# The first pair of column blocks as four plain products of halves

## The reference

```python
def short_conv_mixer(h, w_in, conv_w, w_out):
    b_gate, c_gate, v = jnp.split(h @ w_in, 3, axis=-1)
    u = c_gate * v
    y = lax.conv_general_dilated(u, conv_w[:, None, :], ...)   # width 3, causal, per channel
    return (b_gate * y) @ w_out

h = rmsnorm(x, mix_norm)
x = x + short_conv_mixer(h, conv_w_in, conv_w, conv_w_out)
a = jax.nn.relu(rmsnorm(x, mlp_norm) @ mlp_w1)
x = x + (a * a) @ mlp_w2
```

## Time and profile before

| what | value |
|---|---|
| three timed runs | 1918.24, 1918.30, 1918.65 us, median 1918.3 us |
| the profiled execution: span from the first instruction to the last | 1916.3 us |
| its own time beside the span | not listed apart; the median of the runs is 2.0 us above the span |
| TensorE busy | 1887.0 us (98%) |
| VectorE, ScalarE busy | 1715.8 us (90%), 1022.4 us (53%) |
| granted TensorE clock, mean | 0.998 |

### The profile page before, as it was taken

One profiled execution on the slowest core, in us unless ns is written; L12 is line 12 of the kernel. 1 busy time (PEld: TensorE's weight loads), 2 busy tenths in 40 slices (PEclk: granted clock), 3 DMA queues, 4 the chain that ended last, 5 costly groups with the idle time before them and its releaser, 6 DMA issues.

```text
span 1916.3 us, 22288 instructions
## 1 busy us (share of the span) xinstructions
PE 1887.0 (98%) x8512; PEld 1560.8 (81%) x8512; DVE 1715.8 (90%) x1518; ACT 1022.4 (53%) x1095; POOL 152.9 (8%) x244
## 2 busy tenths in 40 slices
PE   7899999999999999999999999999999999999999
PEld 5678888888888888888888888888888888888887
DVE  7999899898999989989899898998998889888878
ACT  6653655535557476565665756655444333333332
POOL 1100011000011111111111111110000000000000
PEclk9999999999999999999999999999999999999999
DMA  9865659657776975877858678599988878887782
GB/s 357 313 219 164 219 188 363 218 153 270 250 201 245 370 222 182 332 247 227 328 184 332 247 226 328 184 399 399 357 315 348 350 281 312 351 317 278 294 330 115
DMA packets 120698, 527.90 MB, mean 275 GB/s; under 512 B 13072, under 2 KB 17168, under 8 KB 95504
## 3 DMA queue, kind: packets, MB, share of 16 engines
q1 hardware_dynamic: 86176, 401.64, 54.3%
q0 software_dynamic: 34272, 124.80, 21.4%
q10 hardware_dynamic: 144, 0.04, 0.0%
HBM read 433.10 MB, written 93.32 MB: 275 GB/s over the span
## 4 chain that ended last, share of the span: by engine, by line
PE 94%; DMA 2%; DVE 2%; ACT 1%; issue 1%; POOL 0%; SPq 0%; ACTq 0%; DVEq 0%
PE pair L1097 91%; PE pair L1117 2%; DMA act_kept<-act 1%; DMA raw<-in_turns 1%; DVE ring L839 1%; ACT ring L564 0%; DVE raw L833 0%; DVE sum L870 0%; DVE act L796 0%; ACT quads L513 0%; ACT act L549 0%; DVE quads L898 0%; DVE sum_l_mix L870 0%; ACT later L520 0%; ACT x_tok L524 0%
## 5 line engine op out<-in xcount | busy, mean ns | idle before, releaser
L1097 PE MATMUL pair<-ring,act 128*128 128x512 f32 x8064 | 1851.2, 390 | 23.5 <-DVE ring L839 19.1
L1097 PEld LDWEIGHTS pair<-ring,act 128*128 128x128 f32 x8064 | 1510.5, 188 | 341.3 <-issue 25.8
L564 ACT ACTIVATE ring<-raw 128x1024 fp32r<-128x1024 f32 x672 | 712.1, 1061 | 827.6 <-PE pair L1097 561.8
L839 DVE TENSOR_TENSOR ring<-raw,ring 128x1024 fp32r<-128x1024 f32 x672 | 809.9, 1222 | 149.1 <-ACT ring L564 146.3
L833 DVE TENSOR_TENSOR raw<-raw 128x1024 f32<-128x1024 f32 x324 | 382.0, 1221 | 8.0
L448 POOL DMA_DIRECT2D spill<-stage x136 | 78.4, 611 | 474.9 <-ACT stage L668 371.7
L461 POOL DMA_DIRECT2D raw<-in_turns x60 | 53.6, 1047 | 746.6 <-DVE raw L833 746.6
L820 DVE TENSOR_TENSOR stage<-quads,stage 128x1024 fp32r<-128x1024 f32 x68 | 83.1, 1222 | 25.5 <-ACT stage L668 25.0
L870 DVE TENSOR_TENSOR sum<-pair,sum 128x1024 f32<-128x1024 f32 x64 | 78.0, 1219 | 0.0
L668 ACT ACTIVATE stage<-quads 128x1024 fp32r<-128x1024 f32 x68 | 71.5, 1052 | 11.8 <-DVE quads L756 10.2
L590 ACT ACTIVATE sum<-pair 128x1024 f32<-128x1024 f32 x64 | 64.9, 1013 | 0.2 <-PE pair L1097 0.2
(11 more groups left out here) (93 smaller groups left out, 435.4 us busy)
## 6 DMA issues: line engine op xcount, KB each, us to landing
raw<-in_turns SPq DMA_DIRECT2D x192, 1024.0 KB, 7.1
act<-spill SPq DMA_DIRECT2D x282, 512.0 KB, 6.7
spill<-stage POOLq DMA_DIRECT2D x136, 512.0 KB, 9.2
act<-act_kept SPq DMA_DIRECT2D x68, 512.0 KB, 6.7
raw<-in_turns POOLq DMA_DIRECT2D x60, 512.0 KB, 8.4
act_kept<-act POOLq DMA_DIRECT2D x26, 512.0 KB, 9.0
x_tok<-in_x SPq DMA_DIRECT2D x4, 1024.0 KB, 14.5
x<-mixed SPq DMA_DIRECT2D x8, 512.0 KB, 16.1
```

What stands on the lines that cost most here:

```text
L564: nc.scalar.activation(ring[g % RING][:, 0], raw[:, RAW_OF[j], 2 * (s % 2):2 * (s % 2) + 2, :], ACT.Copy).then_inc(hi_ready, 1)
L839: nc.vector.tensor_tensor(ring[g % RING][:, 1], raw[:, RAW_OF[order(v)[s // 2]], 2 * (s % 2):2 * (s % 2) + 2, :], ring[g % RING][:, 0].bit ...
L1097: mm = nc.tensor.matmul(bank, stationary, moving, start=(opens and k == 0 and n == 0), stop=(closes and k == NT - 1 and n == 2))
```

## The change

Turns 0 and 1 (pair 0) become plain: eight products of quadrants each instead of seven, with no sums on either side. A turn then has 8 slots, one for each half of a weight quadrant in the order R11, R12, R21, R22, and every slot serves two left quadrants: 24 matmuls a slot, 192 a turn. The four results stay in the four PSUM pairs over both turns, and ScalarE copies them out (`copy_plain`) during turn 2. The sums of weights, the T3 transfers, the twelve adds and the five copies of pair 0 go away for turns 0 and 1. The summed left factors are still made, since turns 2 and 3 use them, but later in the order. The first slot is made in pieces: x11 and R11 are loaded in two halves each, and ScalarE and VectorE scale and split them by pieces of one k (`split_lead_hi`, `split_lead_lo`, `split_first_hi`, `split_first_lo`). TensorE runs nine matmuls on a tile of ones before its first product.

```diff
+WARM = 9
+PLAIN_TURNS, PLAIN_SLOTS = 2, 8
+L21 = 7
+PLAIN_RAWS = (R11, R12, R21, R22)
+PLAIN_LEFTS = {R11: (L11, L21), R12: (L11, L21), R21: (L12, L22), R22: (L12, L22)}
+PLAIN_BANK = {(0, 0): 0, (1, 0): 2, (0, 1): 3, (1, 1): 1}
 def t3_by_transfer(v):
-    return v < V_OUT + 2 or V_UP <= v < V_DOWN
+    return PLAIN_TURNS <= v < V_OUT + 2 or V_UP <= v < V_DOWN
...
 # SyncE
-            load_x(quad["L11"], 0, 0, x_in["L11"])
-            load_raw(0, R11)
+            for h in range(2):
+                k = slice(2 * h, 2 * h + 2)
+                sp.dma_start(quad["L11"][:, k], xt_v[:, k, 0:HALF]).then_inc((first_x_in, x_in["L11"])[h], 16)
+                sp.dma_start(raw[:, R11, k, :], turns[R11, :, k]).then_inc((first_raw_in, raw_turn_in[R11])[h], 16)
+                if h == 0:
+                    load_x(quad["L21"], 0, 1, x_in["L21"])
+            load_raw(0, R12)
             load_x(quad["L12"], DT // 2, 0, x_in["L12"])
+            load_x(quad["L22"], DT // 2, 1, x_in["L22"])
             load_raw(0, R21)
-            load_x(quad["L21"], 0, 1, x_in["L21"])
-            load_x(quad["L22"], DT // 2, 1, x_in["L22"])
-            load_raw(0, R12)
             load_raw(0, R22)
...
+            for v in range(PLAIN_TURNS):
+                for n, r in enumerate(PLAIN_RAWS):
+                    sp.wait_ge(lo_ready, first_slot(v) + 2 * n + 2)
+                    load_raw(v + 1, r)
+                    if v == 1 and r == R11:
+                        sp.wait_ge(act_lo_ready, direct_done(0, S4))
+                        for t in (0, 1):
+                            load_tokens(t)
...
 # ScalarE
+            def split_lead_hi(name, k):
+                act.wait_ge(first_x_in if name == "L11" and k < 2 else x_in[name], 16)
+                place = act_place(0, {"L11": L11, "L21": L21}[name])
+                nc.scalar.activation(place[:, 0, k, :], quad[name][:, k, :], ACT.Copy,
+                                     scale=cols[:, MIX + k:MIX + k + 1]).then_inc(lead_hi[name], 1)
+            def split_first_hi(k):
+                act.wait_ge(first_raw_in, 16)
+                nc.scalar.activation(ring[0][:, 0, k, :], raw[:, R11, k, :], ACT.Copy).then_inc((first_hi, hi_ready)[k], 1)
+            def copy_plain(n):
+                act.wait_ge(used, 2 * PLAIN_SLOTS - (2 if n < 2 else 0))
+                if n < 2:
+                    act.wait_ge(squared, 1)
+                o = sums_of(0)[(0, 5, 4, 1)[n]]
+                nc.scalar.activation(o[:], pairs[(0, 2, 3, 1)[n]][:], ACT.Copy).then_inc(plain_copied, 1)
...
+            split_lead_hi("L11", 0)
+            split_first_hi(0)
+            split_lead_hi("L11", 1)
+            split_first_hi(1)
+            split_lead_hi("L21", 0)
+            split_lead_hi("L21", 1)
             split_turn_hi(0, 1)
+            for k in (2, 3):
+                split_lead_hi("L11", k)
+            for k in (2, 3):
+                split_lead_hi("L21", k)
+            split_turn_hi(0, 2)
+            split_turn_hi(0, 3)
             direct_hi(0, L12)
+            direct_hi(0, L22)
+            split_turn_hi(0, 4)
+            direct_hi(0, S3)
+            scale_later(0)
+            split_turn_hi(0, 5)
+            scale_later(1)
+            direct_hi(1, L11)
+            split_turn_hi(0, 6)
+            direct_hi(1, L21)
+            square_tokens(2)
+            split_turn_hi(0, 7)
...
+                    if v == PLAIN_TURNS:
+                        if s == 0:
+                            direct_hi(1, S2)
+                            root_of(1)
+                        if s == 1:
+                            copy_plain(0)
+                            copy_plain(1)
+                        if s == 2:
+                            direct_hi(1, S4)
+                        if s == 3:
+                            copy_plain(2)
+                            copy_plain(3)
...
 # VectorE
+            def split_lead_lo(name, k):
+                dve.wait_ge(lead_hi[name], k + 1)
+                place = act_place(0, {"L11": L11, "L21": L21}[name])
+                nc.vector.scalar_tensor_tensor(out=place[:, 1, k, :], in0=quad[name][:, k, :],
+                                               scalar=cols[:, MIX + k:MIX + k + 1], in1=place[:, 0, k, :].bitcast(F32),
+                                               op0=ALU.mult, op1=ALU.subtract).then_inc(lead_lo[name], 1)
...
+            split_lead_lo("L11", 0)
+            split_first_lo(0)
+            split_lead_lo("L11", 1)
+            split_first_lo(1)
+            split_lead_lo("L21", 0)
+            split_lead_lo("L21", 1)
             split_turn_lo(0, 1)
+            for k in (2, 3):
+                split_lead_lo("L11", k)
+            for k in (2, 3):
+                split_lead_lo("L21", k)
+            split_turn_lo(0, 2)
+            scale_x("L12")
+            split_turn_lo(0, 3)
+            scale_x("L22")
             direct_lo(0, L12)
+            direct_lo(0, L22)
+            scale_x("L11")
+            scale_x("L21")
             direct_form(0, 0)
+            split_turn_lo(0, 4)
+            direct_form(0, 2)
+            direct_lo(0, S3)
+            split_turn_lo(0, 5)
...
+                    if v == PLAIN_TURNS and s == 3:
+                        form_weights(v, T2)
+                        form_u(0, 0)
+                        form_u(0, 1)
...
 # TensorE
+            pe.wait_ge(ones_ready, 1)
+            for _ in range(WARM):
+                nc.tensor.matmul(pairs[3][:, 0, 0:P], ones[:], ones[:], start=True, stop=True)
             pe.wait_ge(ones_ready, 2)
+            for v in range(PLAIN_TURNS):
+                for s in range(PLAIN_SLOTS):
+                    r = PLAIN_RAWS[s // 2]
+                    if v > 0 or s > 0:
+                        pe.wait_ge(lo_ready, PLAIN_SLOTS * v + s + 1)
+                    for left in PLAIN_LEFTS[r]:
+                        if v > 0 or left in (L12, L22):
+                            pe.wait_ge(act_lo_ready, direct_done(v, left))
+                        for k in (2 * (s % 2), 2 * (s % 2) + 1):
+                            if v == 0 and s < 2:
+                                pe.wait_ge(lead_lo[{L11: "L11", L21: "L21"}[left]], k + 1)
+                            if v == 0 and s == 0 and left == L11:
+                                pe.wait_ge((first_lo, lo_ready)[k], 1)
+                            for t in range(2):
+                                mm = plain_tile(v, r, left, k, t)
+                    mm.then_inc(used, 1)
```

More of the change, by code:

```diff
@@ L218, in conv_mlp_layer @@
         ones_ready = sem("ones_ready")
-        x_scaled = sem("x_scaled")
-        x_diagonal_scaled = {n: sem(f"x_diagonal_scaled_{n}") for n in ("L11", "L22")}
+        x_scaled = {n: sem(f"x_scaled_{n}") for n in ("L11", "L21", "L12", "L22")}
+        later_scaled = sem("later_scaled")
+        lead_hi = {n: sem(f"lead_hi_{n}") for n in ("L11", "L21")}
+        lead_lo = {n: sem(f"lead_lo_{n}") for n in ("L11", "L21")}
+        first_x_in = sem("first_x_in")
+        first_raw_in = sem("first_raw_in")
+        first_hi = sem("first_hi")
+        first_lo = sem("first_lo")
+        plain_copied = sem("plain_copied")
         squared = sem("squared")
@@ L261, in formed @@
         def formed(v, t):
-            before = sum(3 if t3_by_transfer(w) else 4 for w in range(v))
+            before = sum(3 if t3_by_transfer(w) else 4 for w in range(PLAIN_TURNS, v))
             return 2 * (before + ({T1: 1, T2: 2, T4: 3}[t] if t3_by_transfer(v) else t))
@@ L394, in _ @@
                 load_tokens(t)
-            for v in range(NV - 1):
+            for v in range(PLAIN_TURNS):
[6 more added lines that the diff above has]
+                            load_tokens(t)
+            for v in range(PLAIN_TURNS, NV - 1):
                 after = v + 1
@@ L413, in _ @@
                     elif r is not None:
-                        sp.wait_ge(lo_ready, SLOTS * v + {R12: 10, R22: 12, R21: 14}[r])
+                        sp.wait_ge(lo_ready, first_slot(v) + {R12: 10, R22: 12, R21: 14}[r])
                         load_raw(after, r)
[L416 to L419, removed]
                     if after == V_DOWN and j in (L11, S1, L12, S3):
@@ L875, in form_u @@
                 o, other = ((first, s4), (l22, s1))[half]
-                dve.wait_ge(added, 12 * q + (11, 12)[half])
+                if q == 0:
+                    dve.wait_ge(plain_copied, (3, 4)[half])
+                else:
+                    dve.wait_ge(added, pair_added(q) + (11, 12)[half])
                 dve.wait_ge(norm_step, NORM_X)
@@ new lines, in _ @@
+            direct_form(1, 2)
+            split_turn_lo(1, 2)
+            split_turn_lo(1, 3)
+            split_turn_lo(1, 4)
+            direct_lo(1, L12)
+            direct_lo(1, L22)
+            split_turn_lo(1, 5)
+            direct_lo(1, S3)
+            split_turn_lo(1, 6)
+            split_turn_lo(1, 7)
+            direct_lo(1, S1)
+            direct_form(1, 1)
+            dve.wait_ge(squared, NT)
```

(17 more changed lines are left out.)

263 lines of the change are left out of this document (131 added, 132 removed).

## The result

The changed kernel takes 1909.02 us (four runs, 1908.8 to 1909.13), the one before 1918.47 on the same chip: 9.45 us less. The measured ratio is 0.9947, 95% interval 0.9934 to 0.9959 (the two medians alone give 0.9951): a small gain, clear of the noise. Forecast were 10.4 us less, 1907.9.

What follows compares the result with a forecast made beforehand. The start was taken as bound by the chain weights, sum, high part, low part, the rest by TensorE's matmul count. Turn 2 starting 10.1 us earlier and 0.3 within it made -10.4: 1918.3 became 1907.9, range 1906 to 1913.5.

Steps and rivals of the forecast that it cites:

- TensorE's count: Turns 0 and 1: 384 matmuls at 0.2267 us take 87.04 us if nothing waits; 48 added matmuls cost 10.9 us.
- The first product: Kernel start: with x11 and R11 in halves, the first product begins at 6.9 us, 2.8 earlier.
- The lower end of the range: First product no earlier than 6.2 us, as a small load takes 3.3 us to land; total 1906.4 with no cold matmul.
- The clock: Start of turn 0: half-clock matmuls cost 0 if the nine on ones serve, 1.4 us if they fail; 0.7 taken.
- rival D: Cold start: slow clock costs 2.7 us in place of 0.7, giving 1909.9 us; chance 0.12.
- my bounds: Before the first product: each matmul on ones takes 0.26 to 0.42 us, nine ending at 3.4 to 4.8.
- The slots behind: Ring slots after the first: tightest is slot 5, ready at 32.7 against 34.1 needed, cover 1.4 us.
- Rival A: Turn 0: the feed is late, one wait at each of slots 4 to 7, +4.2 us, 1912.1; chance 0.15.
- The handover: Turn 2, slot 3: `turn_quad` needs `form_u` 6.3 us after the plain turns end, cover 1.9; turn 2 takes 39.89.
- Rivals B and C: Turns 0 and 1: B, half the waits stay, 1915.9 us, chance 0.08; C, weights' transfers set the waits, 1923.9, 0.07.
- The 18.84 us: Time lost in turns 0 and 1 of the kernel before: some 2.8 us clock, 16 waits.

Runs made afterwards that it cites:

- the first kernel with other first loads: Changed kernel with R11's first two k each alone and first on SyncE's queue, x11's half on ScalarE's, eleven matmuls on ones: 1910.49 us.
- whole first loads: Changed kernel with x11 and R11 each loaded whole in one transfer, splitting by pieces kept: 1910.98 us.
- the kernel with 64 matmuls fewer: Changed kernel with one of three matmuls of each product left out in turn 1 (low left part by high weights): 1899.7 us.
- fourteen: Changed kernel with fourteen matmuls on ones in place of nine before the first product: 1907.61 us.
- The kernel with eight sums: Changed kernel with the first sum of left factors done eight times instead of once on VectorE, before slot 4 of turn 0: 1913.63 us.
- the seven products without sums: Kernel before, seven products, with sums of weights and their T3 transfers left out in turns 0 and 1: 1908.61 us, ratio 0.9944.
- on the seven products: Kernel before with x11 and R11 in halves, first slot split by k, x11's scaling moved behind slot 2: 1920.66 us, ratio 1.0011.

## Why the prediction was right

The mechanism held at each step but for two sizes; both erred to the same side, so no large errors cancel in the total.

- *TensorE's count.* 384 matmuls at 0.2267 with no wait behind the first: right, 43.52 in turn 1.
- *The first product*, forecast at 6.9, came at 7.46. The mis-sized term is the transfer of R11's half, 1.2 us behind x11's half; it measured 2.0 (x11's half came 0.15 earlier and the work 0.1 shorter than said). I had halved the time of a whole transfer; in the same stretch the halves moved at 250 GB/s, the whole transfers at 452, on engines nearly as busy. Smaller packets and x21's share of the stretch both fit; they were not separated. +0.56. The lower end of the range took 3.3 us for a small load "whatever its size"; that is not borne out, the 40 KB of column scales took 3.3, 2.9 and, in the first kernel with other first loads, 4.6.
- *The clock*, taken as 0.7, half of 1.4: it cost 1.43, the upper case named there (rival D's mechanism, though not its 2.7). Half of two cases is no mechanism, and the case that came is the one where the nine fail. The question put as open, whether the idle time behind the matmuls on ones undoes them, has the answer that it can: with 2.2 to 3.5 us idle, seven to eleven matmuls ran at half clock in the two traces of the changed kernel and with whole first loads, none in the kernel with 64 matmuls fewer; fourteen, with 0.23 us idle, cost 0.12. +0.73. The price of the matmuls themselves: nine took 4.21 us and fourteen 6.34, so 0.426 for each of the five more, the upper of my bounds. The Trainium skill ("FP8 and Floating Point Precision", TensorE Precision Notes) says that a true 32-bit product takes four passes; the estimate made from it, 0.42, agrees with this trace, which shows the time and not the passes.
- *The slots behind.* Forecast cover at slot 5 was 1.4 us; the trace has slot 5 ready at 31.6 and TensorE there at 36.1, 4.5 us. TensorE came 2.0 later than said, by the first product (0.56) and the clock (1.43); the lists ran 1.1 shorter, as instructions that take 1.22 follow each other at 1.14 when nothing is waited for. Rival A fell: no wait at all. The kernel with eight sums agrees, with 4.7.
- *The handover*, cover 1.9: VectorE's `form_u` ended at 102.3, `turn_quad` started at 104.09, 1.8. Turn 2's 39.89 came out as 39.88. The two lines:
```profile
100.88 1.41 DVE L981 SCALAR_TENSOR_TENSOR sum_first_mix<-sum_first_mix,rstd_sq,sum 128x512 f32<-128x512 f32 x2
104.09 1.03 PE L1261 MATMUL pair<-eye,sum_first_mix 128*128 128x128 f32 x8
```
- *Rivals B and C* fell with the single wait; the seven products without sums show why C had to: with the loads of weights and x as they were (the T3 transfers left out) the greater part of the waits went.
- *The 18.84 us.* The forecast calls 16 of them waits and 2.8 clock. By its rows the clock is 1.4 + 1.1 = 2.5 us; of the rest, the lists name 9.4 us as waits for ring slots and 2.69 as "issue". Some 4.3 stand in neither: TensorE's restart behind each gap is the likely place, which was argued and not tested.

The sum: 94.6 forecast for the start of turn 2, 95.93 measured, 0.56 + 0.73 of it from the two terms. In all 9.1 us: 2.3 from the earlier first product, 6.5 in turns 0 and 1 (17.4 less of waits and half clock, 10.9 more of matmuls), 0.3 in turn 2.

## What to carry to other kernels

An engine that is 98% busy can still be served better by giving it more work, where a scheme that saves matmuls puts a chain of other engines in front of them: here 10.9 us more of matmuls removed 17.4 us of waits and half clock, in the first two turns. Size a start in pieces by transfers of the size that the pieces have, and look at what the pieces push back: on the seven products a first product 2.6 us earlier ended 2.2 us slower. And do not count on warm-up matmuls that leave a gap before the first real one: with the 2.2 to 3.5 us of idle time here, most of the traced executions lost what they had gained.

## What the runs showed of the hardware that was not expected

The same bytes in smaller transfers landed later here. With x11 and R11 whole, R12, the fourth transfer, behind them and x21, was issued at 2.3 and landed 8.9 later, at 11.2; with the halves it was issued at 3.3 and landed 8.7 later, at 12.0, behind the same bytes. On the seven products the rest of R11 came 1.6 us late.

The clock did not do the same in every execution of the same first instructions. After nine matmuls on ones it rose at 4.28 in the repetition of the changed kernel and fell at 7.69, at the start of the products, behind 2.8 us of idle time. In the kernel with 64 matmuls fewer it rose at 5.74 and held over 2.2 us of idle time. In the kernel with eight sums it rose at 5.25, held over 2.5 us of it, and fell at 8.67, four products later:
```profile
7.78:8.67 0.89, 0.89 (x4) 1.00 1.07 423
8.67:12.08 3.41, 3.41 (x10) 0.50 1.01 408
```
